# Layer 0 opens with the pool-input group on rows without shift; scale and shift become columns on turned blocks

## The reference, cut to what matters

```python
for l in range(DEPTH):                       # DEPTH = 2, D_MODEL = 1024, SEQ = 512
    mod = silu(c) @ w_ada[l] + b_ada[l]      # 1 x 6144
    sh1, sc1, g1, sh2, sc2, g2 = jnp.split(mod, 6, axis=-1)
    h = modulate(rmsnorm(x, norm1_g[l]), sh1, sc1)     # x_hat * g * (1 + sc1) + sh1
    x = x + g1 * mixer(h, w_in[l], ...)      # proj = h @ w_in -> q, k, v, g, u, a_ret, a_pool
    h = modulate(rmsnorm(x, norm2_g[l]), sh2, sc2)
    x = x + g2 * moe(h, ...)                 # 16 experts, top 2 of one group
return rmsnorm(x, final_g)
```

## Time and profile before

| | |
|---|---|
| median of 3 runs | 1480.53 us (1475.91, 1480.53, 1480.9) |
| span of the profiled execution | 1475.1 us from its first to its last instruction |
| TensorE busy | 1440.2 us, 98% |
| DVE busy | 1132.6 us, 77% |
| ACT busy | 767.0 us, 52% |
| mean granted TensorE clock | 0.995 |

### The profile page before, as it was taken

The page is one execution under the profiler, slowest core; times in us unless marked ns, Lnnn a source line. Parts: engine busy times, 40 slices in busy tenths (PEclk is TensorE's granted clock), DMA queues, the critical chain, the costliest instruction groups (busy, mean ns, idle before and its releaser), DMA issues.

```text
span 1475.1 us, 18818 instructions
## 1 busy us (share of the span) xinstructions
PE 1440.2 (98%) x6815; PEld 1152.1 (78%) x6815; DVE 1132.6 (77%) x1538; ACT 767.0 (52%) x1102; POOL 151.6 (10%) x139
## 2 busy tenths in 40 slices
PE   7999999999999999999989999999999999999996
PEld 2788877778878878888758888878888778888884
DVE  5774786555669999999977657854345899999998
ACT  4343433222347878777623344242233587778773
POOL 0000001000012211111100000100000122112010
PEclk9999999999999999999999999999999999999998
DMA  9855556455557999999956543642243879999995
GB/s 355 307 184 188 176 196 209 144 175 172 186 218 290 392 362 398 379 382 378 354 205 204 193 133 115 206 138 87 85 172 145 322 293 387 377 380 395 371 373 210
DMA packets 107413, 377.49 MB, mean 256 GB/s; under 512 B 16521, under 2 KB 16713, under 8 KB 106548
## 3 DMA queue, kind: packets, MB, share of 16 engines
q1 hardware_dynamic: 90864, 331.39, 61.3%
q0 software_dynamic: 15200, 40.62, 7.6%
q10 hardware_dynamic: 1252, 4.22, 0.9%
HBM read 361.32 MB, written 34.64 MB: 268 GB/s over the span
## 4 chain that ended last, share of the span: by engine, by line
PE 80%; DVE 13%; DMA 2%; ACT 2%; issue 2%; DVEq 1%; SPq 0%; ACTq 0%; POOLq 0%; POOL 0%
PE ps L1786 24%; PE ps L1788 23%; PE ps L1787 23%; DVE w_lo L1528 4%; DVE w_lo_more L1528 2%; PE ps L1871 2%; PE ps L2049 1%; DMA gate_row<-mod_rows 1%; PE ps L2098 1%; PE ps L1940 1%; DVE xgT_lo L1514 1%; ACT w_hi L837 1%; DVE y_out L1551 1%; PE ps L1944 1%; DMA raw<-w 1%
## 5 line engine op out<-in xcount | busy, mean ns | idle before, releaser
L1008 DVE TENSOR_TENSOR w_lo<-raw,w_hi 128x1024 fp32r<-128x1024 f32 x132 | 161.4, 1224 | 212.7 <-ACT w_hi L652 211.5
L652 ACT ACTIVATE w_hi<-raw 128x1024 fp32r<-128x1024 f32 x132 | 139.1, 1058 | 333.2 <-PE ps L1788 332.5
L1528 DVE TENSOR_TENSOR w_lo<-raw,w_hi 128x1024 fp32r<-128x1024 f32 x184 | 217.1, 1218 | 2.2 <-DMA gate_row<-mod_rows 1.3
L1786 PE MATMUL ps<-w_hi,hT_lo 128*128 128x512 f32 x512 | 206.9, 404 | 3.2 <-DVE hT_lo L1111 2.5
L1528 DVE TENSOR_TENSOR w_lo_more<-raw,w_hi_more 128x1024 fp32r<-128x1024 f32 x176 | 207.9, 1218 | 1.3 <-ACT w_hi_more L837 0.4
L1788 PE MATMUL ps<-w_hi,hT_hi 128*128 128x512 f32 x512 | 200.0, 391 | 0.0
L1787 PE MATMUL ps<-w_lo,hT_hi 128*128 128x512 f32 x512 | 199.6, 390 | 0.0
L837 ACT ACTIVATE w_hi<-raw 128x1024 fp32r<-128x1024 f32 x184 | 187.4, 1057 | 10.0 <-DMA raw<-w 5.4
L837 ACT ACTIVATE w_hi_more<-raw 128x1024 fp32r<-128x1024 f32 x176 | 178.9, 1056 | 8.4 <-DMA raw<-w 6.3
L1786 PE MATMUL ps<-hT_hi,w_lo 128*128 128x512 f32 x320 | 130.5, 408 | 0.0
L1788 PE MATMUL ps<-hT_hi,w_hi 128*128 128x512 f32 x320 | 125.0, 390 | 0.0
(11 more groups left out here) (286 smaller groups left out, 2632.1 us busy)
## 6 DMA issues: line engine op xcount, KB each, us to landing
raw<-w SPq DMA_DIRECT2D x590, 512.0 KB, 6.1
h_rows<-h POOLq DMA_DIRECT2D x8, 1024.0 KB, 4.9
ahead<-w SPq DMA_DIRECT2D x4, 2048.0 KB, 11.9
x_state<-x POOLq DMA_DIRECT2D x2, 2048.0 KB, 10.3
y_rows<-x_in ACTq DMA_DIRECT2D x4, 1024.0 KB, 11.9
x<-x_state POOLq DMA_DIRECT2D x4, 1024.0 KB, 7.1
pair_early<-y_rows SPq DMA_DIRECT2D x4, 1024.0 KB, 6.8
x<-x_in SPq DMA_DIRECT2D x4, 512.0 KB, 14.1
```

Source lines behind the costliest of these rows:

```text
L652: act.activation(w_hi[:, q % W_SLOTS], stream_piece(l, q, r), ACT.Copy).then_inc(w_hi_ready, 1)
L1008: v.tensor_tensor(w_lo[:, q % W_SLOTS], stream_piece(l, q, r), w_hi[:, q % W_SLOTS], ALU.subtract).then_inc(raw_used, 1)
L1528: v.tensor_tensor(ring_lo(e * EXP + n), expert_piece(e, n), ring_hi(e * EXP + n), ALU.subtract).then_inc(raw_used, 1)
L1786: pe.matmul(dst, a_lo, b_hi, start=start, stop=False)
```

## The change

Layer 0 takes its groups in the order u, q, k, v0, v1 (all else unchanged). The u group runs on the turned rows times the scale alone; the shift is added to the turned rows afterwards, before the q group. Retention comes after the fifth group in both layers, which is v1 in layer 0. x is no longer stored to `x_state` in layer 0; it is loaded again from the input. `rope` and the small first buffers move to another region, `first_w` has four slots instead of two. The core of the diff:

```diff
+ORDER = [["u", "q", "k", "v0", "v1"] + NAMES[5:]] + [NAMES] * (DEPTH - 1)
+HEADS_AFTER = 4
-FIRST_W = 2
+FIRST_W = 4
```

SP's first loads:

```diff
+            def column_half_load(a, j, part, semaphore):
+                cols = slice(256 * part, 256 * part + 256)
+                sp.dma_start(raw[:, j].rearrange("p (i n) -> p i n", i=2)[:, :, cols], ...).then_inc(semaphore, 16)
+            def first_q_load(j):
+                sp.wait_ge(first_used, 3)
+                sp.sem_inc(landed[W_SLOTS + j], 16)
+                first_load(PRE + stored_piece(0, W_SLOTS + j), W_SLOTS + j)
+            for t in range(NT - 1):
+                x_load(t)
+            column_half_load(2, 0, 0, left_landed[0])
+            x_load(NT - 1)
+            for j in range(1, ADA_PIECES):
+                column_half_load(2, j, 0, left_landed[j])
+            first_w_load(0)
+            for j in range(ADA_PIECES):
+                column_half_load(2, j, 1, landed[j])
+            first_w_load(1)
+            for j in range(ADA_PIECES):
+                first_load(ADA_PIECES * 3 + j, ADA_PIECES + j)
+            first_w_load(2)
+            first_w_load(3)
+            sp.wait_ge(first_used, 2)
+            for j in range(ADA_PIECES):
+                first_load(j, j)
+            first_q_load(0)
+            first_q_load(1)
+            for j in range(ADA_PIECES):
+                sp.wait_ge(column_used, j + 1)
+                first_load(ADA_PIECES + j, j)
+            first_q_load(2)
+            first_q_load(3)
+            sp.wait_ge(column_used, 2 * ADA_PIECES)
```

ACT's new steps:

```diff
+            def first_hi(kb):
+                act.wait_ge(first_cols_ready, (1, 1, 2, 2, 3, 3, 3, 3)[kb])
+                scale = first_cols[:, 2 + kb // 4, kb % 4:kb % 4 + 1]
+                unit_hi_half(0, "h1", kb, hT_hi[:, kb], scale=scale)
+                act.activation(scaled[:, kb], ps[:, 4 + (UNIT0["h1"] + kb) % 2], ACT.Copy, scale=scale).then_inc(unit_free, 1)
+            def shifted_high(kb):
+                act.wait_ge(first_cols_ready, 4 + kb // 4)
+                act.wait_ge(w_used, w_done(0, kb // 2))
+                act.activation(hT_hi[:, kb], scaled[:, kb], ACT.Identity, bias=...).then_inc(shifted_hi, 1)
```

DVE's new steps:

```diff
+            def first_normed(t):
+                inverse_deviation(0, t)
+                v.tensor_scalar(x[:, t], x[:, t], x_rs[:, t:t + 1], None, ALU.mult).then_inc(h_ready, 1)
+            def first_low(kb):
+                v.wait_ge(unit_free, unit_value(0, "h1", kb) + 2)
+                v.tensor_tensor(hT_lo[:, kb], scaled[:, kb], hT_hi[:, kb], ALU.subtract).then_inc(first_lo, 1)
+            def shifted_low(kb):
+                v.wait_ge(shifted_hi, kb + 1)
+                v.scalar_tensor_tensor(hT_lo[:, kb], scaled[:, kb], first_cols[...], hT_hi[:, kb], ALU.add, ALU.subtract
+                                       ).then_inc(shifted_lo, 1)
```

TensorE's new steps:

```diff
+            def column_sums(a, acc, n):
+                pe.wait_ge(column_summed, n)
+                for i in range(4):
+                    one = pe.matmul(ps[:, 7, 4 * a + i:4 * a + i + 1], ada_acc[:, acc, i * P:(i + 1) * P], k("ones")[:, 0:1], ...)
+                one.then_inc(first_sum, 1)
```

In `group(l, g)`, for each piece j and tile t, and in GpSimd's layer 0:

```diff
+                        if l == 0 and name == "q" and t == 0:
+                            pe.wait_ge(shifted_lo, 2 * j + 2)
+                            if j == 1:
+                                column_sums(1, 0, 2)
...
-                    pool.wait_ge(first_used, PRE)
-                pool.dma_start(x_state, x[:].rearrange("p t d -> p (t d)")).then_inc(x_saved, 16)
+                    pool.wait_ge(acc_ready, 2)
```

More of the change, by code:

```diff
@@ new lines, in first_shift, with column_products @@
+            def first_shift(n, a):
+                v.wait_ge(first_sum, n)
+                v.tensor_tensor(first_cols[:, a], ps[:, 7, 4 * a:4 * a + 4], first_turned[:, a, 0], ALU.add
+                                ).then_inc(first_cols_ready, 1)
+            def column_products(j, slot, turn, acc):
+                v.wait_ge(landed[slot], 16 * turn)
+                for i in range(2):
+                    piece = raw[:, slot, 512 * i:512 * i + 512]
+                    c = cond[:, 2 * j + i:2 * j + i + 1]
+                    if j == 0 and i == 0:
+                        one = v.tensor_scalar(ada_acc[:, acc], piece, c, None, ALU.mult)
+                    else:
+                        one = v.scalar_tensor_tensor(ada_acc[:, acc], piece, c, ada_acc[:, acc], ALU.mult, ALU.add)
+                    if i == 1:
+                        one.then_inc(column_used, 1)
+                    last = v.drain()
+                if j == ADA_PIECES - 1:
+                    last.then_inc(column_summed, 1)
@@ L1694, in _ @@
                     norm_lo(l, "h1", 3)
-                for q in range(LAST["O0"] + 1):
+                for q in range(0 if l else W_SLOTS, LAST["O0"] + 1):
                     g, j = piece_at(q)
-                    during(l, NAMES[g], j)
+                    during(l, ORDER[l][g], j)
                     ada_pieces(l, q)
@@ new lines, in first_second_scale @@
+            def first_second_scale():
+                for c in range(8):
+                    j, i = divmod(c, 2)
+                    if i == 0:
+                        pe.wait_ge(landed[ADA_PIECES + j], 16)
+                    if c == 0:
+                        pe.wait_ge(first_part_ready, 2)
+                    quadrant = slice(32 * (c % 4), 32 * (c % 4) + 32)
+                    mm = pe.matmul(ps[quadrant, 6], cond_wide[:, c], raw[:, ADA_PIECES + j, 512 * i:512 * i + 512],
+                                   start=c < 4, stop=c >= 4)
+                mm.then_inc(first_used, 1)
@@ new lines, in first_second_fold, with first_fold @@
+            def first_second_fold():
+                pe.wait_ge(first_part_ready, 3)
+                for i in range(4):
+                    one = pe.matmul(ps[:, 7, 12 + i:13 + i], first_part[:, i * P:(i + 1) * P], k("fold")[:, 0:1],
+                                    start=True, stop=True)
+                one.then_inc(first_sum, 1)
+            def first_fold(part):
+                pe.wait_ge(first_part_ready, part + 1)
+                for i in (2 * part, 2 * part + 1):
+                    one = pe.matmul(ps[:, 7, 8 + i:9 + i], first_part[:, i * P:(i + 1) * P], k("fold")[:, 0:1],
+                                    start=True, stop=True)
+                one.then_inc(first_sum, 1)
```

416 lines of the change are left out of this document (196 added, 220 removed).

## The result

The changed kernel takes 1484.59 us (median of 6 runs, 1483.88 to 1487.94) where the kernel before, run beside it, takes 1478.8 (6 runs, 1475.91 to 1480.9): ratio 1.005, 95% interval 1.0033 to 1.0066. It is slower: the medians are 5.8 us apart, and the ratio, taken over all runs, stands for 7.4 us, just at the half per cent that counts as a difference here. The forecast of 1484.3 lies 0.3 us beside the median, but partly by luck: it rested on a base of 1480.53, and the change cost 5.8 to 7.4 where it said 3.8.

What follows compares the result with a forecast made beforehand. TensorE, busy 98% of the span, was taken as the bound. Start -2.2, clock +1.7, columns -0.9, turned blocks -0.5, folds and sums +1.6, waits +3.8 gave +3.75 unrounded: 1484.3 us from 1480.53, range 1478 to 1489.

Steps and rivals of the forecast that it cites:

- The wait between u and q: Before q's first product TensorE waits 2.4 us, until 57.6, for ACT to read u's first bank behind the shift columns.
- no rival: Holes close: 1478.3 us, chance 0.15; clock stays low until q: 1497.4, 0.10; lead of the loads lost: 1486.5, 0.05.
- The second wait: Before piece 1 of q TensorE waits 1.9 us for DVE's right-half shift sums, ready at 65.0.
- the prediction's own marks: Signs include first product at 20 to 22 us, last q read near 82.6; a wait at retention would show it wrong.
- The second fall of the clock: A clock fall in the wait at 55 us costs nothing, since q's piece 0 then only fills the second wait.
- Narrow products: Small f32 products in folds and new sums: about 0.25 us each, bounds 0.11 and 0.5 moving the mark -2.5 and +4.0.
- Start: Opening before the first product: loads, deviations and scale columns let it start at 21.0 us, 2.2 ahead of before.
- Clock: At the first product, after about 3 us without work, the first 3.4 us run at 1.2 GHz, costing 1.7 us.
- Work in the u group: TensorE's products, column sums, turned blocks, narrow products and waits end the u group at 55.2 us; shift columns at 52.8.
- the 7.0: All TensorE waits from first product to the end of the second group, in us, against 3.2 before.
- Retention: v1 directly ahead of retention costs nothing: ACT's four bank reads finish with 1.0 us to spare.
- The halves: Eight 256 KB loads of the scale column; the page's 2.1 us later mark was left out of the sum.

Runs made afterwards that it cites:

- the early reads: Two runs from the changed kernel: ACT reads u's first two banks early, with the other two also moved earlier (1488.59 us) or left in their old place (1489.73 us).
- first early read: Changed kernel with ACT reading u's banks 0 and 1 before the first shifted block, banks 2 and 3 after the second: 1488.59 us, ratio 1.0078.
- the one with four edits: Changed kernel plus early read of two banks, fillers, constants first and right half of shift by TensorE: 1480.01 us, ratio 1.001.

## Why the prediction was right, and where it was off

**Mechanism: right in the main.** The wait between u and q stood where it was put, with its releaser, and the clock was at half in the first products; no rival took place. The second wait was covered by the slow clock in the changed kernel, and shows, ended by DVE, as 1.65 and 2.92 us in two of the experiments. Three of the prediction's own marks were missed: the first product came at 22.13 and not by 22, the last read at 85.41 and not near 82.6, and there is a wait at retention. Waits of 0.41, 0.23, 0.99 and 0.20 us in the u group answer to 0.5, 0.4, 1.25 and 0.5. DVE's chain from the shift columns to the second sums took 12.5 us (55.4 to 67.9), forecast 12.2. The columns moved to TensorE, the early reads and the whole scale column show from three sides that this chain carries the mark.

**The second fall of the clock costs nothing, as said.** "since piece 0 of q then only fills the second wait": with the clock down TensorE reached the sums as DVE ended; with the clock up it waited 1.65 there, and the clock fell behind that wait instead.

**Narrow products: right.** Four one-column sums with the step behind them take 0.92 (54.17 to 55.09), 0.23 each, forecast 0.25; two take 0.47 (28.89 to 29.36). The bounds beside it are mis-added: for 14 such products, 0.11 and 0.5 us each move the mark by -2.0 and +3.5, not by -2.5 and +4.0.

**Start: off by 1.1 us.** The step that failed put ACT free at 9.5 and kept the landing of the constants as before. The row tiles go ahead on SP's queue, the constants on another one came 0.9 later, ACT was free at about 10.3, the last row tile was scaled at 17.05 instead of 16.5, and the first product was 1.1 late. Some 0.4 of that is the clock, which the step had at full rate up to the first product; with the clock up by then, the same stretch was 0.4 shorter in two experiments. Constants first gave back 2.0.

**Clock: off by 0.5, and by 0.9 with the start.** 2.2 us instead of 1.7: nearly the whole block of twelve ran slow. The cause was argued wrongly in part: the prediction made it fall in the hole before the first product, where it had been at half since the first column products. In three other kernels (first early read, right half of shift by TensorE, whole scale column) it was up by then and did fall in that hole, of 3.1 to 3.2 us.

**Work in the u group: about 1 us short.** The shift columns are there at 55.4 instead of 52.8; 1.6 of the 2.6 are the two terms above. The rest I attribute, without an experiment, to each change between products and narrow work: the first product of a block takes 0.31 to 0.34 to the next start instead of 0.227, seven times from 29.75 to 55.09, or 0.7 in all, and a block turned ahead of a fold takes 0.61 (28.28 to 28.89) instead of 0.44. The step that let this slip is the one that counts the waits before as 3.2: that is a remainder, and TensorE's timeline of before lists only 0.48 of it as a wait. Such changes are in the remainder, and none is in the 7.0 set against it.

```profile
25.96 0.50 PE L1786 MATMUL ps<-w_hi,hT_lo 128*128 128x512 f32 x1 [0.48 <-DVE w_lo L1008]
```

The three make 2.6 of the 2.85 by which the mark is later; the rest is the 0.3 of the chain.

**Retention: "nothing, with 1.0 to spare" was wrong.** It cost 0.5 in the profile. The step counted ACT's eight reads of v1 and TensorE's scores, but not the `y_rows` loads that ACT issues between those reads and `state`. The wait follows the time of the last three issues: none where they took 2.05 or 2.73 us (first early read, right half of shift by TensorE), 0.25 at 2.92, 0.47 at 3.13, 0.86 at 3.53, 1.06 at 3.73. None of the edits touches these issues, so the 0.5 is one draw from 0 to 1.1. The old order is not free of it: in the kernel before without fillers four issues took 3.56 us and TensorE waited 0.17.

**The halves: right to leave the page's rule out.** The eight halves landed 8.5 us (median) after issue, the whole pieces of the same opening 8.1, and TensorE never waited for one. The Trainium skill, "DMA: Bandwidth & Descriptors", "Measured", has 138 GB/s for 64 KB and 341 for 1 MB; by the lower figure they would have been 10 us late in all, an estimate from that page, and the trace does not agree for halves that queue behind each other. They are not quite free all the same: in the windows from 10 to 18 us the queues moved 356 to 383 GB/s with the halves, and 408 to 421 in the kernel that loads the column whole.

**The total: right by a shifted base.** By its own terms the change costs 7.1 (6.6 and 0.5) in the profile; the medians show 5.8, the ratio 7.4.

## What to carry to other kernels

When several waits hang on one chain of another engine, find that chain and count its length; removing the wait that shows first only moves it, and here made things worse because the clock then fell in an uncovered place. Give work to the engine that waits, at the place where it waits (column products or fillers of 3 us ahead of the first product), and not before something that the chain needs. When a load moves to the head of one queue, ask what small transfers on the other queues it delays, and count the transfers that an engine issues itself between two of its steps.

## What the runs showed of the hardware

- **The same wait, another clock.** After 2.46 us of idle TensorE fell to half in the changed kernel (0.50 at 62 to 64 us) and not with the whole scale column (1.00 at 61 to 63), where 1.65 us did it later. It stayed at half for 3.4 us in the changed kernel, for 6.8 in the one that reads two banks early. Behind a filler block and a wait of 1.79 us it stayed up in the kernel with fillers alone and fell from 22.75 us on in the one with four edits. A price for a wait is therefore a range. The Trainium skill, "TensorE: Matmul & The Clock Gate", "HAM oscillation — how this bites in real kernels", tells that in a kernel whose TensorE waits for loads between bursts each burst starts slow; the traces agree behind most of these waits (2.46, 2.92) and not behind that of the whole scale column (2.46).
- **The granted clock is not always in the record.** At 22 us it reads 1.00 in the changed kernel while products start every 0.43 us; in the kernel with the whole scale column it reads 0.50 at the same rate. Where the record has not fallen yet, only the starts tell.
- **A scale of 1024 columns by one number for each partition.** `tensor_scalar` on 128x1024 took 0.75 us where the forecast bounded it by 0.48 at half the width and 1.29 for the form with two operands.
- **Issues on ACT's queue.** Three issues of `y_rows` took ACT 2.05 to 3.73 us from run to run, and TensorE's wait at retention grew with them from 0 to 1.06 us.
- **A small row that lands late.** `gate_row` landed 8.1 us after its issue in the trace of before and 10.4 in that of the changed kernel, and kept DVE waiting 1.0 and 3.3 us at the same place. The 3.9 us behind it are more than half of what the whole change costs, so a single pair of profiles would have misled.
